# Sums of squares of the heads as two rounded matmuls in place of one in full precision

## The reference, cut to what matters

```python
def l2norm(x):
    return x * lax.rsqrt(jnp.sum(x * x, axis=-1, keepdims=True) + EPS)
...
    q = l2norm(q.reshape(b, t, DN_HEADS, DN_HEAD_K).astype(jnp.float32)) * (DN_HEAD_K ** -0.5)
    k = l2norm(k.reshape(b, t, DN_HEADS, DN_HEAD_K).astype(jnp.float32))
...
    o = rmsnorm(o, out_gain) * jax.nn.silu(zf)
...
    q = rmsnorm(q.reshape(b, t, DF_HEADS, 2, DF_HEAD_QK), q_gain) * (DF_HEAD_QK ** -0.5)
    k = rmsnorm(k.reshape(b, t, DF_HEADS, 2, DF_HEAD_QK), k_gain)
...
    o = rmsnorm(o, out_gain).astype(jnp.float32) * (1.0 - lambda_init)
```

## Time and profile before

| | |
|---|---|
| median of 3 runs | 2025.61 us (2025.31 to 2026.02) |
| the profiled execution, its time | 2024.86 us |
| its span | 2023.1 us |
| PE busy | 1992.5 us, 98% of the span |
| DVE, ACT, POOL busy | 864.0, 734.1, 936.2 us |
| mean granted clock of PE | 0.998 |
| matmul records with `square` and `const`, 128x512 | 58, 599 ns mean |

### The profile page before, as it was taken

The page is one execution under the profiler, slowest core; times in us unless marked ns, Lnnn a source line. Parts: engine busy times, 40 slices in busy tenths (PEclk is TensorE's granted clock), DMA queues, the critical chain, the costliest instruction groups (busy, mean ns, idle before and its releaser), DMA issues.

```text
span 2023.1 us, 30232 instructions
## 1 busy us (share of the span) xinstructions
PE 1992.5 (98%) x11374; PEld 1703.2 (84%) x11374; DVE 864.0 (43%) x1507; ACT 734.1 (36%) x1113; POOL 936.2 (46%) x1220
## 2 busy tenths in 40 slices
PE   8999999999999999999999999999999999999998
PEld 6788777799999999788998888888888888888887
DVE  7844675922222224994442244333334452222112
ACT  4643554432222224534444242333333332232222
POOL 5432112555445565553332635454544665555564
PEclk9999999999999999999999999999999999999999
DMA  5211101222222323221111322222222222223232
GB/s 178 94 63 43 42 32 43 73 84 93 93 87 90 104 93 105 76 94 61 63 64 42 122 72 89 73 99 74 81 81 76 92 93 93 99 89 102 94 104 84
DMA packets 49898, 168.68 MB, mean 83 GB/s; under 512 B 6416, under 2 KB 8592, under 8 KB 49808
## 3 DMA queue, kind: packets, MB, share of 16 engines
q1 hardware_dynamic: 46336, 161.37, 23.4%
q10 hardware_dynamic: 3472, 6.03, 0.9%
HBM read 165.29 MB, written 2.10 MB: 83 GB/s over the span
## 4 chain that ended last, share of the span: by engine, by line
PE 87%; DVE 9%; ACT 2%; issue 1%; DMA 1%; DVEq 0%; ACTq 0%
PE slot L2055 86%; DVE ix_score L1860 1%; DVE top L1856 1%; DVE ix_score L1877 1%; DVE square L1813 1%; DVE x_lo L1830 0%; DVE xt L1822 0%; DMA ix_rot<-rotations 0%; PE slot L2492 0%; PE slot L2230 0%; PE slot L2195 0%; DVE ak L1815 0%; DMA small<-small_in 0%; ACT mixed_hi L945 0%; DVE aq L1815 0%
## 5 line engine op out<-in xcount | busy, mean ns | idle before, releaser
L2569 POOL TENSOR_TENSOR w_lo<-w_raw,w_hi 128x256 fp32r<-128x256 f32 x1216 | 936.0, 802 | 1076.2 <-ACT w_hi L824 816.6
L2055 PE MATMUL slot<-x_hi,w_hi 128*128 128x264 f32 (+1 forms) x1864 | 642.9, 345 | 0.2 <-DVE x_lo L1830 0.2
L2055 PE MATMUL slot<-x_hi,w_lo 128*128 128x264 f32 (+1 forms) x1864 | 629.8, 338 | 0.0
L2055 PE MATMUL slot<-x_lo,w_hi 128*128 128x264 f32 (+1 forms) x1864 | 628.1, 337 | 0.0
L2055 PEld LDWEIGHTS slot<-x_hi,w_hi 128*128 128x128 f32 x1864 | 351.2, 188 | 46.6 <-issue 7.6
L2055 PEld LDWEIGHTS slot<-x_lo,w_hi 128*128 128x128 f32 x1864 | 350.5, 188 | 38.6
L2055 PEld LDWEIGHTS slot<-x_hi,w_lo 128*128 128x128 f32 x1864 | 351.3, 188 | 37.5 <-issue 1.4
L824 ACT ACTIVATE w_hi<-w_raw 128x1024 fp32r<-128x1024 f32 x215 | 225.3, 1054 | 320.5 <-PE slot L2055 312.0
L2055 PE MATMUL slot<-f_hi,w_hi 128*128 128x264 f32 (+2 forms) x550 | 173.7, 316 | 0.0
L2055 PE MATMUL slot<-f_hi,w_lo 128*128 128x264 f32 (+2 forms) x550 | 173.5, 315 | 0.0
L2055 PE MATMUL slot<-f_lo,w_hi 128*128 128x264 f32 (+2 forms) x550 | 173.1, 315 | 0.0
(11 more groups left out here) (348 smaller groups left out, 2862.0 us busy)
## 6 DMA issues: line engine op xcount, KB each, us to landing
w_raw<-weights SPq DMA_DIRECT2D x303, 512.0 KB, 3.2
h<-x_t ACTq DMA_DIRECT2D x4, 512.0 KB, 6.4
dec<-decays ACTq DMA_DIRECT2D x4, 264.0 KB, 3.0
const<-consts SPq DMA_DIRECT2D x1, 576.0 KB, 7.1
at_rot<-rotations ACTq DMA_DIRECT2D x1, 528.0 KB, 5.0
ix_rot<-rotations ACTq DMA_DIRECT2D x1, 528.0 KB, 6.9
rt_rot<-rotations ACTq DMA_DIRECT2D x1, 528.0 KB, 3.9
w_raw<-weights SPq DMA_DIRECT2D x2, 256.0 KB, 4.2
```

Of the source, the lines that this page charges most:

```text
L2055: return nc.tensor.matmul(out, lhsT, rhs, start=start, stop=stop)
L2569: nc.gpsimd.tensor_tensor(w_lo[j][:, piece], w_raw[j][:, piece], w_hi[j][:, piece].bitcast(F32), ALU.subtract).then_inc(s_lo, 1)
```

## The change

22 of the 24 sums (all but `LATE_HEADS`) take squares that are split like every dense operand. ACT squares the head twice, exactly (into a float32 buffer) and with a rounded output (the high part); POOL subtracts (`square_lows`) and gives the low part; PE multiplies both with ones of type float32r, two rounded matmuls that add up. The ones and the block ones are rounded once by ACT into `const_r` and `const1_r`, which lie over the constants themselves; matmuls that stay in full precision read them as float32. The first eight sums have two sets of buffers in the space of `dv`, the later ones a single set in the space of `square` (`square_pair`), so that ACT waits there for the sum before.

POOL's program, a loop before, is written out for the blocks of the first stage in the order of ACT's: at each point first the weight blocks, then the squares. The output heads of chunks 1 and 2 move from points 38 and 56 to 61 and 64.

```diff
-HO_POINT = {**{n: POINTS * (n + 1) + 2 for n in range(NQ - 1)}, **{4 + j: DF_START + 8 * j + 15 for j in range(3)}}
+HO_POINT = {0: POINTS + 2, 1: 61, 2: 64, **{4 + j: DF_START + 8 * j + 15 for j in range(3)}}
 LATE_HEADS = [3, 7]
+HEAD_SUMS = 8
+SPLIT_SUMS = 2 * HEAD_SUMS + 8 - len(LATE_HEADS)
...
+        def square_pair(n):
+
+            if n < HEAD_SUMS:
+                at = 2 * (n % 2)
+                return dv_r[:, at, :], dv[:, at + 1, :], dv_r[:, at + 1, :]
+            return square_r[:, 0, 0:T], square[1][:, 0:T], square_r[:, 1, 0:T]
...
             def squares(srcs):
                 for src in srcs:
-                    q = made["sq"]
-                    if q >= KD + 2:
-                        act.wait_ge(s_sqd, q - KD - 1)
-                    w = src.shape[-1]
-                    nc.scalar.activation(square[q % 2][:, 0:w], src, ACT.Square).then_inc(s_sq, 1)
+                    n = made["sq"] - KD
+                    if n > HEAD_SUMS:
+                        act.wait_ge(s_sqd, n)
+                    elif 2 <= n < HEAD_SUMS:
+                        act.wait_ge(s_sqd, n - 1)
+                    shape = heads if len(src.shape) == 3 else lambda ap: ap
+                    hi, exact, _ = square_pair(n)
+                    A.own(nc.scalar.activation(shape(exact), src, ACT.Square))
+                    nc.scalar.activation(shape(hi), src, ACT.Square).then_inc(s_sq, 1)
                     made["sq"] += 1
...
+            act.wait_ge(s_const, 16)
+            nc.scalar.activation(K_rounded("ones"), K("ones"), ACT.Copy).then_inc(s_ones, 1)
             act.wait_ge(s_eps, 1)
             rsqrt(("norm", 0), 1.0 / D, T)
...
+            act.wait_ge(s_small, 48)
+            nc.scalar.activation(K_rounded("ones64"), K("ones64"), ACT.Copy).then_inc(s_ones, 1)
             act.wait_ge(s_g, 1)
...
-            def sums(key, n, w, ones="ones"):
+            def sums(key, ones="ones"):
 
                 ps = begin(key)
...
+                n = done["sq"]
+                if n < SPLIT_SUMS:
+                    pe.wait_ge(s_sqlo, n + 1)
+                    hi, _, lo = square_pair(n)
+                    mm(ps[:, 0:T], K_rounded(ones), hi, True, False)
+                    m = mm(ps[:, 0:T], K_rounded(ones), lo, False, True)
+                else:
+                    pe.wait_ge(s_sq, KD - SQUARES_VECTOR + n + 1)
+                    m = mm(ps[:, 0:T], K_rounded(ones).bitcast(F32), square[n - SPLIT_SUMS][:, 0:T], True, True)
+                m.then_inc(s_sqd, 1)
+                done["sq"] += 1
...
+            def square_lows(count):
+
+                for _ in range(count):
+                    n = made["sq"]
+                    hi, exact, lo = square_pair(n)
+                    pool.wait_ge(s_sq, KD - SQUARES_VECTOR + n + 1)
+                    nc.gpsimd.tensor_tensor(lo, exact, hi.bitcast(F32), ALU.subtract).then_inc(s_sqlo, 1)
+                    made["sq"] += 1
+            lows(BLOCK[("qkv", 8)] + RING - 1)
+            square_lows(2)
+            for j in range(9, 13):
+                lows(BLOCK[("qkv", j) if j < 12 else ("ab",)] + RING - 1)
+                square_lows(sum(i + 2 < HEAD_SUMS for i in norms_after(j)))
+            for p in range(FIRST_POINT, LAST_POINT):
+                lows(BLOCK[ASIDE_DENSE[0]] + aside_blocks(p + 1) + RING - 1)
+                square_lows(len(norm_at(p, -1)) + sum(p == first - 1 for first in HO_POINT.values()))
+            assert made["sq"] == SPLIT_SUMS
+            lows(-(-made["w"] // RING) * RING - 1)
+            with pool.Fori(made["w"] // RING, BLOCKS_PADDED // RING) as i:
```

More of the change, by code:

```diff
@@ L560, in build @@
         h = sb("h", [P, KD, TT])
+        with ExitStack() as scope:
+            const_r = sb("const_r", [P, N_KEPT], F32R, scope)
         const = sb("const", [P, N_KEPT])
@@ L587, in build @@
             dqk = fb("dqk", [P, 8, T])
+            with ExitStack() as after:
+                dv_r = fb("dv_r", [P, NQ, T], F32R, after)
             dv = fb("dv", [P, NQ, T])
@@ L612, in build @@
             lamt = fb("lamt", [P, 8])
+            with ExitStack() as after:
+                const1_r = fb("const1_r", [P, N_CONST - N_KEPT], F32R, after)
             const1 = fb("const1", [P, N_CONST - N_KEPT])
@@ L685, in build @@
         s_sqd = sem("square_used")
+        s_sqlo = sem("square_lo_made")
+        s_ones = sem("ones_rounded")
         s_acc = sem("squares_added")
@@ L2284, in _ @@
             for i in LATE_HEADS:
-                sums(("ho", i), 1, T)
+                sums(("ho", i))
             for j in range(4):
@@ L2357, in half_sum @@
                     pe.wait_ge(s_acc, SQUARES_BEFORE_LAST + 2 * (KD - 1) + (a + 1 if last else 0))
-                    m = mm(ps[:, 0:256], K("ones"), square[0 if last else 1][:, a * 256:a * 256 + 256], not last, last)
+                    m = mm(ps[:, 0:256], K_rounded("ones").bitcast(F32), square[0 if last else 1][:, a * 256:a * 256 + 256], not last, last)
                     if last:
@@ L2570, in low, with lows @@
                                         ALU.subtract).then_inc(s_lo, 1)
-            pool.wait_ge(s_halfhi, 1)
-            for j in range(RING):
-                for p in range(LO_PIECES):
-                    if j or p == LO_PIECES // 2:
-                        pool.wait_ge(s_hi, j + 1)
-                    low(j, p)
-            with pool.Fori(1, BLOCKS_PADDED // RING) as i:
+            made = {"w": 0, "sq": 0}
+            def lows(upto):
+                while made["w"] <= upto:
+                    b = made["w"]
+                    for p in range(LO_PIECES):
+                        if (b, p) == (0, 0):
+                            pool.wait_ge(s_halfhi, 1)
+                        elif p == (0 if b else LO_PIECES // 2):
+                            pool.wait_ge(s_hi, b + 1)
+                        low(b % RING, p)
+                    made["w"] += 1
+            def square_lows(count):
[16 more added lines that the diff above has]
+            with pool.Fori(made["w"] // RING, BLOCKS_PADDED // RING) as i:
                 for j in range(RING):
```

50 lines of the change are left out of this document (24 added, 26 removed).

## The result

The changed kernel took **2039.3 us** (median of 6, 2037.7 to 2040.4) against 2025.7 us (2025.3 to 2026.4) for the kernel before: a ratio of 1.0066, 95% interval 1.0055 to 1.0076, or 13.6 us more. The forecast was 2026.8 us, and its range ended at 2033.0 us.

What follows compares the result with a forecast made beforehand. PE was taken as the bound, busy 98% of the span. Terms -0.2 - 5.7 + 4.0 + 2.8 + 0.3 gave +1.2 us, 2026.1 against the profiled execution; with 0.75 for the median, 2026.8 us, range 2021.5 to 2033.0.

Steps and rivals of the forecast that it cites:

- Step 1: Eight delta-head sums, 72 to 97 us: first pair 2.04 later, other pairs save 2.46, plus 0.2 for collisions: -0.2 us.
- Step 2: 14 sums inside the recurrence, 105 to 340 us: gross gain 5.7 us against 4.0 us of PE stalls for POOL's subtraction.
- Step 3: Stretch from 211 to 229 us, bound by ACT and DVE: PE's wait for `dn_y` ends 1.5 us later; loss 2.8 us.
- Step 4: Moved output-head sums cost 0.3 us; rounding the ones, POOL's written-out program and SP's DMAs cost nothing.
- such brushes: Delta-head sums: small delays like head 3's low part coming at 82.6 when PE wants it at 82.5; 0.2 us charged.
- Rival B: POOL and DVE block each other, lengthening weight blocks and subtractions: 9.4 us more, 2036.2 us; half strength 2031.5; chance 0.22.
- Rival C: PE's clock falls in the delta-head sums, with 0.5 us of work between 72.0 and 76.0: 2.6 us, 2029.4 us; chance 0.10.
- The gross gain: On PE, each split sum saves 0.41 us as two rounded matmuls; 22 sums give 9.0 us.
- The subtraction: POOL's 128x512 subtraction giving the low part, behind the weight block: taken as 1.4 us, bounds 0.70 and 1.93.

Runs made afterwards that it cites:

- all_ones_early: The changed kernel with ACT's rounding of `ones64` moved ahead of its first two head squares: 2039.1 us.
- one_square: The changed kernel with `ones64` rounded early, ACT making only the rounded square, PE counting it twice, no exact square or low part: 2022.4 us.
- no_split_ones_early: The changed kernel with all 22 sums back to single full-precision matmuls and `ones64` rounded ahead of the first head squares: 2027.8 us.
- sub_first_ones_early: The changed kernel with `ones64` rounded early and POOL's subtraction ahead of its point's weight block instead of behind it: 2040.3 us.
- heads_back: The changed kernel with `ones64` rounded early and the first three mixed heads' sums at their old points: 2040.0 us.
- filled: The changed kernel with `ones64` rounded early and unneeded PE matmuls, 36 before the first low-part wait, 40 before the `xt` wait: 2039.9 us.

## Why the prediction was wrong

The sum gave +1.2 us, and the profiled execution came out 14.3 us longer. Of the 13.1 us between them, 4.0 are step 1's, 6.3 belong to steps 2 to 4, 1.4 to the start and 1.4 to the part behind 350 us.

- **Step 1, -0.2 us.** This is the step that failed first. By the trace it cost 3.8 us (norm 0 to `xt`), and 4.7 in `all_ones_early`. The first pair was forecast to cost 2.0 us; at the second PE was 3.0 us behind, of it 0.9 for matmuls at half pace, and it got 0.8 and 0.7 back by the third and the fourth, as forecast. What had no term is the wait for `xt`, 2.81 us. "I charge 0.2 us for such brushes" was wrong: the brush was taken as POOL's queue, and was in truth DVE's products at 1.38 us in place of 0.73 and 0.82, 10 of them in 30 us. Rivals B and C were both at work here.
- **The gross gain, 9.0 us.** The price of a sum is as forecast: pairs of rounded matmuls take 0.23 each, and the eight sums of `one_square` bring PE 2.9 us forward between norm 0 and `xt` (+1.1 to -1.8), where 8 x 0.41 = 3.3 was forecast. Over all 22 only 5.4 us arrive. The term was mis-sized because it counted each saving inside the recurrence as if PE were the bound there. In the profiled execution of `one_square` (2.7 us over its median) the 14 sums there give 0.1 us in all: from `xt` to 350 us PE takes 254.9 us, and 255.0 in `no_split_ones_early`. Most stretches between sums are 0.4 us shorter, and 2.5 us come back around `dn_y`, where the clock also fell.
- **Step 2, stalls of 1.8, 1.5 and 0.7.** Measured 2.0, 1.3 and 1.3 us, at the places named; 4.65 for 4.0. This part was right, and yet taking the stalls away (`sub_first_ones_early`) gave nothing back.
- **Step 3, +2.8 us.** The wait for `dn_y` was to end 1.5 us later and last over 3 us; it lasted 3.37 and ended 1.55 later (PE was 9.95 us behind the kernel before at 210 us, and 11.50 at 225.53). Right, but the run of eight behind it took 0.9 us more at the lower clock, and all up to the next sum 1.4, which the sum didn't have. That the wait lasted over 3 us was luck in part: in `all_ones_early` it was 1.78.
- **Step 4, +0.3 us.** Two of its prices of nothing failed. The moves cost 1.1 us by the trace and 1.7 by the medians, where 0.3 was charged; at one place it shows why, since the 0.86 us taken from before `dn_y` lay under ACT's chain. And the rounding of `ones64`, "ahead of which ACT idles or runs free of PE: nothing", is waited for by PE behind two `rsqrt` in ACT's program: 3.9 us where nothing else hides it, nothing in the changed kernel. The prediction looked at the copy's length (0.29 us), not at where it stands. POOL's written-out program was nothing, as forecast.
- **The subtraction, 1.4 us.** Mostly it took 1.25 to 1.33, so 0.1 us less than charged. The Trainium skill, GPSIMD Engine Reference, section "3.1 Elementwise — side-by-side cycle accounting", gives GpSimd about 2.6 cycles for each element of a two-input operation; at the 1.2 GHz of that section's own example 512 elements are an estimate of 1.11 us, and the trace has 0.16 more. Beside DVE the subtraction took up to 1.81, and DVE's instruction beside it 1.66 where its like two rows further took 0.69; it stands ahead of `mx`, for which PE then waits 1.45 us:

```profile
114.61 1.27 POOL L2628 TENSOR_TENSOR square_r<-square,square_r 128x512 fp32r<-128x512 f32 x1
...
224.14 1.81 POOL L2628 TENSOR_TENSOR square_r<-square,square_r 128x512 fp32r<-128x512 f32 x1
...
224.84 1.66 DVE L1620 TENSOR_TENSOR dn_inv<-dn_n,const 128x512 f32<-128x512 f32 x1
```

- **Rival B, POOL and DVE block each other, 2036.2 at full strength, chance 0.22.** This was the likeliest case and was undersold. It priced POOL's side (longer subtractions and blocks), while the cost lay in DVE's: 6.9 us with nobody on PE waiting for a subtraction. The Trainium skill's exclusive lock (SBUF — State Buffer, section "🔬 SBUF: two separate sides") would hold a DVE product of 0.7 us for up to a whole subtraction of 1.27, so up to 2.0; the rows show 1.38 on average and 1.8 at most, the longest beside a subtraction that started 0.03 us before it. The trace agrees with the rule; what the prediction missed is whose time it takes.
- **Rival C, the clock.** It fell below 1.00 between 66 and 100 us, which the prediction named as a sign that it is wrong. "After the idle 1.97 us at 225 the granted clock stayed at 1.00" was one execution. The same gap may bring the clock down or not: behind the stall of 2.0 us at 125 it was 1.00 in the changed kernel and 0.90 in `all_ones_early` (118 to 135 us). The eleven timed executions of the kernel with the moves alone run from 2024.99 us at a mean granted clock of 0.999 to 2029.53 at 0.996. By the rows above the falls behind the first pair, `xt` and `dn_y` are some 4 us of the changed kernel's profiled execution (0.9, 1.6 and 1.4); the prediction had given one such fall 2.6 us and a chance of 0.10.

The 1.4 us behind 350 us are the clock's too. From the attention product there to the next norm's sums (420.75 in the changed kernel) the changed one and `all_ones_early` take 57.6 us, the kernel before 56.0, with dense matmuls 0.43 us apart behind short gaps at 368 us and a granted clock of 0.74 from 370 to 376. `heads_back`, which makes all the split sums too, takes 56.0, and `no_split_ones_early`, which makes none, 56.9: it goes with the execution, and no run ties it to the splitting.

What stays open: how much of the +5.3 us for PE's wait is the wait and how much the clock behind it (`filled` can't tell, as said), why the clock falls after one gap and not after a like one, and the 1.4 us at the start.

## What to carry to other kernels

Before pricing a helper's new instruction at its length, list what every other engine reads beside it: here an operation on GpSimd that TensorE didn't wait for cost about as much as the waits for it (6.9 and 5.3 us). Price a one-time setup copy by its place in its engine's program and by the wait that was added for it, not by its length. And where a chain through other engines sets the pace, neither a shorter matmul ahead of it nor a removed stall counts; look for the wait that grows by the same amount. If you fill a gap to hold the clock up, read first how long one filler takes and what else calls the helper that holds them.

## What the runs showed of the hardware

- VectorE's 128x512 instructions with two SBUF inputs took 1.38 us on average beside GpSimd's 128x512 subtractions and 0.73 to 0.82 without them, while those with a PSUM input kept 0.75 us. One with a single SBUF input went from 0.43 to 1.44 (`dn_decay` in `filled`). GpSimd's own subtraction went from 1.27 to at most 1.84 us (`all_ones_early`).
- After gaps on TensorE of 1.8 to 4.2 us the dense matmuls behind often started 0.43 us apart for some 1 to 4 us, and then 0.23 again; after others of that length they did not, and the gap of 2.0 us at 125 did one in `all_ones_early` and the other in the changed kernel, whose streams are alike there. One such fall cost 1.2 us where nothing behind it gave the time back, and another nothing, ahead of a wait for another engine. With the gaps filled by matmuls nobody needs, the granted clock stayed at 1.00 (72 to 118 us).
- One program's executions spread by 4.5 us (0.2%) with the mean granted clock, 0.999 to 0.996, so that a profile of a single execution can be off its median by 2.7 us (`one_square`: profiled 2025.1, median 2022.4).
